# A pair's two expert half matrices brought by one transfer instead of two, in a one-core MoE layer

## What is computed

```python
h = layer_norm(DEEPNORM_ALPHA * h + mix, ln1_g[l], ln1_b[l])
ffn = grouped_moe(h, w_router, b_router, w1[l], w3[l], w2[l])   # 32 experts, 2 per token
...
hb = jax.nn.silu(xb @ w1[e]) * (xb @ w3[e])      # w1, w3: (32, 2048, 512)
return hb @ w2[e]                                # w2: (32, 512, 2048)
```

## Time and profile before

| | us |
|---|---|
| three runs | 1289.26, 1292.16, 1293.69 |
| their median | 1292.16 |
| the profiled execution | 1291.66 |
| its span (first to last instruction) | 1289.9 |
| PE busy | 1240.5 (96%) |
| DVE busy | 445.7 (35%) |
| ACT busy | 321.5 (25%) |
| moved by DMA | 472.28 MB |

### The profile page before, as it was taken

The page is one execution under the profiler, slowest core; times in us unless marked ns, Lnnn a source line. Parts: engine busy times, 40 slices in busy tenths (PEclk is TensorE's granted clock), DMA queues, the critical chain, the costliest instruction groups (busy, mean ns, idle before and its releaser), DMA issues.

```text
span 1289.9 us, 15356 instructions
## 1 busy us (share of the span) xinstructions
PE 1240.5 (96%) x6679; PEld 715.7 (55%) x6679; DVE 445.7 (35%) x635; ACT 321.5 (25%) x545; POOL 9.8 (1%) x18
## 2 busy tenths in 40 slices
PE   6999999999999999999999998989999999999997
PEld 5989989988744544444444444434443444444532
DVE  7788997755420203132130211102020202111026
ACT  6344343533331211111211111111121111111212
POOL 2000000000000000000000000000000000000000
PEclk9999999999999999999999999999999999999998
DMA  8565555597799999999999999999999999999996
GB/s 287 185 216 176 186 176 192 174 351 259 290 418 422 417 425 428 423 428 428 427 428 428 427 428 427 428 427 427 429 427 428 426 429 428 428 426 427 425 411 236
DMA packets 70999, 472.28 MB, mean 366 GB/s; under 512 B 7962, under 2 KB 8546, under 8 KB 41234
## 3 DMA queue, kind: packets, MB, share of 16 engines
q1 hardware_dynamic: 70498, 470.48, 89.7%
q10 hardware_dynamic: 432, 0.79, 0.2%
HBM read 469.14 MB, written 2.10 MB: 365 GB/s over the span
## 4 chain that ended last, share of the span: by engine, by line
PE 75%; DMA 21%; DVE 2%; SPq 1%; issue 0%; ACT 0%; DVEq 0%
PE psum L886 29%; DMA ring<-in_w_dram 19%; PE psum L644 9%; PE psum L671 9%; PE psum L931 8%; PE psum L808 7%; PE psum L607 5%; PE psum L610 2%; DMA area_g<-in_w_dram 2%; PE psum L844 2%; PE psum L845 1%; PE psum L966 1%; DMA area_a<-in_x_dram 1%; PE psum L873 1%; PE psum L785 1%; DVE area_d L1409 0%
## 5 line engine op out<-in xcount | busy, mean ns | idle before, releaser
L886 PE MATMUL psum<-ring,area_c 128*64 128x512 f32 x1504 | 339.3, 604 | 19.9 <-DMA ring<-in_w_dram 19.9
L886 PEld LDWEIGHTS psum<-ring,area_c 128*64 128x64 f32 x1504 | 110.3, 139 | 229.7 <-issue 228.7
L1251 ACT ACTIVATE area_c<-psum,gain 128x128 f32<-128x128 f32 x256 | 96.5, 457 | 294.5 <-PE psum L808 294.5
L1811 DVE TENSOR_TENSOR area_a<-area_a,psum 128x512 f32<-128x512 f32 x56 | 38.3, 685 | 358.9 <-PE psum L845 358.9
L931 PE MATMUL psum<-ring,area_d 128*64 128x512 f32 x704 | 154.8, 594 | 2.8 <-DMA ring<-in_w_dram 2.6
L1417 DVE TENSOR_TENSOR w_low<-ring,w_high 128x2048 fp32r<-128x2048 f32 x56 | 128.3, 2291 | 67.4 <-ACT w_high L1098 67.1
L1098 ACT ACTIVATE w_high<-ring 128x2048 fp32r<-128x2048 f32 x56 | 107.3, 1917 | 149.1 <-PE psum L644 44.0
L808 PE MATMUL psum<-one_hot,area_b 128*128 128x128 f32 x1024 | 124.9, 278 | 0.8 <-DVE one_hot L1738 0.8
L808 PEld LDWEIGHTS psum<-one_hot,area_b 128*128 128x128 f32 x1024 | 118.0, 192 | 13.1 <-issue 12.2
L1795 DVE TENSOR_TENSOR y_low<-psum,y_high 128x512 fp32r<-128x512 f32 x64 | 42.7, 687 | 234.6 <-ACT y_high L1260 234.6
L886 PE MATMUL psum<-slot,area_c 128*64 128x512 f32 x272 | 120.5, 595 | 2.5 <-DMA area_g<-in_w_dram 2.5
(11 more groups left out here) (224 smaller groups left out, 1073.2 us busy)
## 6 DMA issues: line engine op xcount, KB each, us to landing
ring<-in_w_dram SPq DMA_DIRECT2D x112, 2048.0 KB, 25.7
ring<-in_w_dram SPq DMA_DIRECT2D x52, 1024.0 KB, 9.6
ring<-in_w_in_dram SPq DMA_DIRECT2D x40, 1024.0 KB, 5.1
slot<-in_w_dram SPq DMA_DIRECT2D x19, 2048.0 KB, 25.1
area_g<-in_w_dram SPq DMA_DIRECT2D x19, 2048.0 KB, 29.9
ring<-in_w_out_dram SPq DMA_DIRECT2D x16, 1024.0 KB, 5.2
slot<-in_w_dram SPq DMA_DIRECT2D x10, 1024.0 KB, 9.4
area_g<-in_w_dram SPq DMA_DIRECT2D x10, 1024.0 KB, 11.5
```

What stands on the lines that cost most here:

```text
L886: mm = pe.matmul(psum[i * CAP:(i + 1) * CAP, j // UNITS, :], gathered[:, kk, i * CAP:(i + 1) * CAP], w[i][:, k, :], start=kk == 0, stop=kk ...
L1251: ins = act.activation(gathered[:, k, :], psum[:, 2 + g % 2, k % 4 * P:(k % 4 + 1) * P], ACT.Identity, scale=gain[:, 0, k:k + 1], bias=gai ...
```

## The change

The two half matrices of a pair are brought by one DMA instruction, with an access pattern of 128 partitions x 2 experts x 4096 (or 2048) elements on both sides. For that, the two buffers of each pair of slots have to lie at one distance within one tensor:

- `slot0` and `area_g` become the two rows of a new tensor `front`; `area_g` leaves its place behind `area_d`.
- slots 2 and 3 become `ring` rows 0 and 5 (a step of five rows), where slot 2 was row 5 and slot 3 row 0. In the loads ahead, 2 and 3 trade places for that, so that the same memory is filled at the same moments.
- slots 4 and 5, 6 and 7 are neighbouring rows of `ring`.

A pair now signals by one semaphore, that of its even slot; PE waits for that one, except in the first fill of the slots, which is still made by single quarters. The last three pairs wait for 16 instead of 32 on the second quarters' semaphore.

```diff
+        front = sb("front", [P, 2, UNIT_FLOATS])
+        slot0 = front[:, 0, :]
...
-        area_g = sb("area_g", [P, 2, D])
...
-        slots = [slot0[:], flat_g, ring[:, SLOTS - 3, :]] + [ring[:, i, :] for i in range(SLOTS - 3)]
+        slots = [slot0, flat_g, ring[:, 0, :], ring[:, SLOTS - 3, :]] + [ring[:, i, :] for i in range(1, SLOTS - 3)]
+        slot_pairs = (front[:], ring[:, 0:SLOTS - 2:SLOTS - 3, :], ring[:, 1:3, :], ring[:, 3:5, :])
...
+        def pair_of(m, r=None):
+
+            both = slot_pairs[slot_of(m) // 2]
+            return both if r is None else both[:, :, r * D:(r + 1) * D]
...
+            def half_matrices(j, pair):
+
+                part = j // 2
+                return (w1, w3, w2)[part // 2][0, 2 * pair:2 * pair + 2].rearrange(
+                    "i (h p r) d -> h p i (r d)", h=2, p=P)[part % 2]
...
-            def load_expert_unit(m, j, pair):
-
-                sp.dma_start(slots[slot_of(m)], half_matrix(j, pair)).then_inc(loaded[slot_of(m)], 16)
+            def load_two(m, j, pair):
+
+                sp.dma_start(pair_of(m), half_matrices(j, pair)).then_inc(loaded[slot_of(m)], 16)
+
+            def load_two_quarters(m, r, j, pair, signal):
+
+                sp.dma_start(pair_of(m, r), half_matrices(j, pair)[:, :, r * D:(r + 1) * D]).then_inc(signal, 16)
...
-            for both, held in refills:
+            for m, held in refills:
                 for r in range(2):
                     unit_used(held // STEP_UNITS, held % STEP_UNITS, r)
-                    for m in both:
-                        load_quarter(m, r)
+                    load_two_quarters(m, r, m % STEP_UNITS, m // STEP_UNITS, loaded[slot_of(m)])
...
-            for m in range(SPLIT_FILLS, LAST):
+            for m in range(SPLIT_FILLS, LAST, 2):
                 unit_used((m - SLOTS) // STEP_UNITS, (m - SLOTS) % STEP_UNITS)
-                load_expert_unit(m, m % STEP_UNITS, m // STEP_UNITS)
...
                 for r in range(2):
-                    for i in range(2):
-                        sp.dma_start(quarter_of(m + i, r), half_matrix(j + i, pair)[:, r * D:(r + 1) * D]).then_inc(
-                            loaded[slot_of(m + i)] if r == 0 else second_rows[(m - LATE) // 2], 16)
+                    load_two_quarters(m, r, j, pair, loaded[slot_of(m)] if r == 0 else second_rows[(m - LATE) // 2])
...
                         if n in HELD:
                             pe.wait_ge(held_loaded[HELD.index(n)], 16 * 2)
-                        else:
+                        elif n < SLOTS or n % 2 == 0:
                             pe.wait_ge(loaded[slot_of(n)], arrivals(n))
```

More of the change, by code:

```diff
@@ L108, in hybrid_layer @@
         ring = sb("ring", [P, SLOTS - 2, UNIT_FLOATS])
-        slot0 = sb("slot0", [P, UNIT_FLOATS])
+        front = sb("front", [P, 2, UNIT_FLOATS])
+        slot0 = front[:, 0, :]
         area_a = sb("area_a", [P, TT, D])
@@ L139, in hybrid_layer @@
         flat_a = area_a[:].rearrange("p t d -> p (t d)")
-        flat_g = area_g[:].rearrange("p t d -> p (t d)")
+        flat_g = front[:, 1, :]
+        area_g = flat_g.rearrange("p (t d) -> p t d", t=2)
         def quarter(flat, n):
@@ L379, in load_quarter @@
                     held_loaded[HELD.index(m)] if m in HELD else loaded[slot_of(m)], 16)
-            ahead = {UNITS * N_IN + 4 + i: at for i, at in enumerate(((2, 0), (2, 1), (7, 1), (0, 0), (0, 1), (1, 0), (1, 1)))}
+            ahead = {UNITS * N_IN + 4 + i: at for i, at in enumerate(((3, 0), (3, 1), (7, 1), (0, 0), (0, 1), (1, 0), (1, 1)))}
             for u in range(N_UNITS):
@@ L426, in unit_used @@
                     sp.wait_ge(y_ready, NC * it + NC)
-            for freed, quarters in ((UNITS - 3, ((3, 0),)), (UNITS - 2, ((3, 1), (6, 0), (6, 1))),
+            for freed, quarters in ((UNITS - 3, ((2, 0),)), (UNITS - 2, ((2, 1), (6, 0), (6, 1))),
                                     (UNITS - 1, ((4, 0), (5, 0))), (UNITS, ((4, 1), (5, 1), (7, 0), (HELD[0], 0), (HELD[0], 1)))):
@@ L438, in _ @@
             N_HALVES = PAIRS * STEP_UNITS
-            refills = [((m, m + 1), m - SLOTS) for m in range(SLOTS, HELD[0], 2)]
-            refills += [((m, m + 1), m - HELD[0]) for m in range(STEP_UNITS, SLOTS + STEP_UNITS, 2)]
-            refills += [((m, m + 1), m - SLOTS) for m in range(SLOTS + STEP_UNITS, SPLIT_FILLS, 2)]
-            for both, held in refills:
+            refills = [(m, m - SLOTS) for m in range(SLOTS, HELD[0], 2)]
+            refills += [(m, m - HELD[0]) for m in range(STEP_UNITS, SLOTS + STEP_UNITS, 2)]
+            refills += [(m, m - SLOTS) for m in range(SLOTS + STEP_UNITS, SPLIT_FILLS, 2)]
+            for m, held in refills:
                 for r in range(2):
                     unit_used(held // STEP_UNITS, held % STEP_UNITS, r)
-                    for m in both:
-                        load_quarter(m, r)
+                    load_two_quarters(m, r, m % STEP_UNITS, m // STEP_UNITS, loaded[slot_of(m)])
             sp.wait_ge(logits_ready, 1)
@@ L451, in _ @@
             LAST = N_HALVES - 2 * SLOTS
-            for m in range(SPLIT_FILLS, LAST):
+            for m in range(SPLIT_FILLS, LAST, 2):
                 unit_used((m - SLOTS) // STEP_UNITS, (m - SLOTS) % STEP_UNITS)
-                load_expert_unit(m, m % STEP_UNITS, m // STEP_UNITS)
-            for n in range(SLOTS - 2):
+                load_two(m, m % STEP_UNITS, m // STEP_UNITS)
+            for n in range(0, SLOTS - 2, 2):
                 unit_used(PAIRS - 2, n)
                 if n < HALF // 2:
-                    load_expert_unit(LAST + n, n, PAIRS - 1)
+                    load_two(LAST + n, n, PAIRS - 1)
                 else:
-                    load_expert_unit(LAST + n, n + UNITS, PAIRS - 2)
+                    load_two(LAST + n, n + UNITS, PAIRS - 2)
             def load_pair(m, j, pair):
                 for r in range(2):
-                    for i in range(2):
-                        sp.dma_start(quarter_of(m + i, r), half_matrix(j + i, pair)[:, r * D:(r + 1) * D]).then_inc(
-                            loaded[slot_of(m + i)] if r == 0 else second_rows[(m - LATE) // 2], 16)
+                    load_two_quarters(m, r, j, pair, loaded[slot_of(m)] if r == 0 else second_rows[(m - LATE) // 2])
             unit_used(PAIRS - 2, SLOTS - 2)
@@ L819, in arrived @@
                             pe.wait_ge(held_loaded[HELD.index(n)], 16 * 2)
-                        else:
+                        elif n < SLOTS or n % 2 == 0:
                             pe.wait_ge(loaded[slot_of(n)], arrivals(n))
                 elif LATE <= m < LATE + 6:
-                    pe.wait_ge(second_rows[(m - LATE) // 2], 16 * 2)
+                    pe.wait_ge(second_rows[(m - LATE) // 2], 16)
                 return [[quarter_of(n, r) for r in range(2)] for n in pair]
```

## The result

In 15 runs of each, the changed kernel took 1294.09 us (median; 1292.07 to 1296.33) and the kernel before 1292.85. One execution of the kernel before took 2956.10 us and is left out of the ratio. The ratio is 1.0016, 95% interval 1.0008 to 1.0023: slower, by 2.1 us by the ratio and by 1.2 us between the two medians, clear of noise, though within the 0.3% that the prediction calls no change. The forecast was 1290.9, 1.3 us on the other side of the median that it started from (1292.16). The profiled execution took 1293.05 us, its span is 1290.8.

A forecast was written before the change was run, and what follows sets the result against it. The DMA stream of expert weights was taken to bound the kernel. 1291.66 less 1.2 for fewer transfers, all other terms 0, gave 1290.5; a median 0.5 above the profiled execution made it 1290.9 us, range 1286.5 to 1295.5.

The forecast's parts named there:

- no change: Whole kernel: time stays within 0.3%, 3.9 us, of the kernel before; chance 0.73.
- The bound: Expert stage: the DMA stream from about 355 to 1249 us sets the end; a per cent of rate is 9 us.
- The transfer's share: DMA stream: 0.012 us per transfer, from 0.084 less eight packets' 0.072; 103 transfers fewer save 1.2 us.
- The packet's price: DMA stream: each data packet on an engine costs 0.0090 us besides its bytes.
- the lower bound: DMA stream: fewer transfers save 0, if all of the 0.084 us per transfer belongs to packets.
- When they are there ... Price 0: PE's waits for pairs: one semaphore instead of two, the dropped one being the earlier; price 0.
- Moved buffers: Buffer places: same places filled at the same moments, PE, DVE and ACT instruction counts unchanged in first 350 us; price 0.
- general warning: Rate stays, end moves over 4 us: first 350 us or tail depends on buffer places or SP at the full queue.
- Rival B: DMA stream: each packet alternating between experts' matrices 4 MiB apart pays 0.0090 us more, 14.8 us slower, 1306; chance 0.14.
- SP's waits: SP's queue: waits for the same event, then issues one instruction instead of two; price 0.
- the full queue: SP's issues around 1220 us: a doubled transfer may wait longer, but the stream doesn't stop; price 0, bounds 0 and 2 us.
- The sign: Whole kernel: faster by 1.2 us, from fewer transfers in the DMA stream.

The follow-up runs named there:

- experiment 11: Changed kernel with 50 instructions added on PE in the branch never taken, and SPLIT_FILLS = 20 instead of 32: 1295.51 us, ratio 1.0032.
- run 2: Kernel before, transfers untouched, with 206 instructions added on PE's queue in the branch never taken: 1293.33 us, ratio 1.0015.
- run 4: Changed kernel's buffer places, but one transfer per half matrix again, with single semaphores and waits as in the kernel before: 1291.39 us, ratio 0.9994.
- run 1: Changed kernel with 50 instructions added on PE's queue in the branch never taken: 1292.22 us, ratio 0.9998; run again later: 1291.00 us, ratio 1.0003.
- experiment 3: Changed kernel with the 50 PE waits put back and executed, as second waits on the even slot's semaphore: 1291.95 us, ratio 0.9993.
- run 5: Changed kernel with 242 instructions added on PE in the branch never taken: 1291.64 us, executed once.
- run 6: Changed kernel with 250 instructions added on PE in the branch never taken: 1295.60 us, executed once.

## Why the prediction was right or wrong

**The bound: right.** The stream sets the pace of the expert stage. Every price that touched it came through to the end: 11.0 us for smaller packets and 4.1 us for larger ones, and a queue that ran dry for some 3 us in a run that was 4.1 us slower.

**The transfer's share: too large.** I took 1.2 us, from 0.084 less eight packets, as a difference of rates known to perhaps a half per cent (my estimate: with quarters alone the rows of experiment 11 have 423 and 417 GB/s in neighbouring stretches). The packet's price was well read (0.0090, measured 0.0092, 0.0098 and 0.0092). The remainder, 0.012 us a transfer, was within the error of the three rates; eight packets at 0.0092 leave 0.010, and the direct comparison with the same packets leaves nothing to be seen. The three runs of the changed kernel with its tail in place have ratios 0.9998, 1.0003 and 0.9993. The traces say the same: from the issue of the first expert quarter to the end of the last combining matmul it takes 940.7 to 942.4 us in the three kernels with single transfers (before, runs 2 and 4), and 940.7 to 943.9 us in six traces with pairs (after, run 1 twice, runs 3, 5 and 6). The saving is 0 within about 1 us, and the lower bound would have been the nearer value.

**"When they are there ... Price 0": here is the step that failed.** The argument on time was right: PE doesn't need the second wait, and executing it costs nothing (experiment 3). But 50 instructions were taken out of PE's program, and I asked only what they cost to execute and not what stands behind them. They shift the code, and with it the borders of the blocks in which it is fetched; behind the branch one of these came to lie where nothing covers the fetch, and PE stood still for 1.59 us. This cost 1.9 us, as much as the whole loss. In "Moved buffers" I wrote that instruction counts stay in the first 350 us, and looked no further. The text had only a general warning for this (an end that moves though the rate stays), and put it down to places of buffers or to SP.

**Rival B: right to be doubted.** No loss by alternating between matrices 4 MiB apart is seen: 427 GB/s with and without. The rule of the Trainium skill (DMA: Bandwidth & Descriptors, Latency and other measured facts) that the prediction set beside it, of rows 4 MiB apart from partition to partition, isn't contradicted; it doesn't apply to this pattern, in which the partitions' rows stay 16 KB apart.

**The other zeros: right.** SP's waits, the full queue and the buffers' places cost nothing that these runs can see (experiments 1, 3 and 4). They can't tell less than about 1 us.

**The numbers.** 1294.09 lies in the range and within the 0.3%, where I had 0.73. That is luck in part: the range was wide enough for a loss that none of its terms contains. The sign, and the place of the loss, were not foreseen by any of the cases. Of the 3.2 us between forecast and median, 1.9 are the tail and 1.2 the saving that didn't come.

## What to carry to other kernels

In a DMA queue that stays full, count packets and not transfers: here it was 0.009 us for each packet on each engine, from 8 to 32 KB, and nothing to be seen for joining two transfers whose packets stay as they are. And when an edit takes instructions out of an engine that ends the kernel, look at what lies behind the next taken branch: when the time moves by 2 us and the profile shows an idle piece called "issue" that is new, ask whether the cause is where the code lies. Some instructions in a branch that is never taken test this in one run.

## What I had not expected of the hardware

- After a taken branch, PE could go on behind the first border of a block of instructions only 6.4 to 6.5 us after its last matmul ahead of the branch. The 4.4 us in which it waited for ACT covered two thirds of that: one packet, 2.2 us in which none came, and the start of the second.
- A row of 32 KB went as a single packet, and the stream rose to 430 GB/s. A kernel that uses it with the right weights would need both experts' full matrices in SBUF before it starts on either (the two are multiplied side by side), with buffers for only two such sets; this wasn't tried.
- Cutting a transfer by partitions into four about halved the rate of a stream (224 for 427 GB/s from 500 to 700 us, 285 after that), with every DMA engine shown as busy. The DMA share in the profile is no sign that a stream runs at its best.
